# RMS norms of a hybrid decoder layer: squares summed in f32 on VectorE and two ones products a norm in the own tiles, where eight were

## The reference

```python
def rms_norm(x, g):
    y = x * lax.rsqrt(jnp.mean(x * x, axis=-1, keepdims=True) + EPS)
    return y * g

f1 = swiglu(rms_norm(h, ffn1_norm_pre), ffn1_w_in, ffn1_w_out)
h = h + 0.5 * rms_norm(f1, ffn1_norm_post)
u = rms_norm(h, mix_norm_pre)
...                       # u @ w_in: dilated windows A, sliding window B, memory attention M
merged = g_a * (o_a @ w_o_a) + g_b * (o_b @ w_o_b) + g_m * (o_m @ w_o_m)   # g: sigmoid(u @ w_gate + b)
h = h + rms_norm(merged @ w_out, mix_norm_post)
f2 = swiglu(rms_norm(h, ffn2_norm_pre), ffn2_w_in, ffn2_w_out)
h = h + 0.5 * rms_norm(f2, ffn2_norm_post)
```

## Time and profile before

| | us |
|---|---|
| runs (three) | 3924.27 median, 3917.88 to 3935.54 |
| the profiled execution | 3930.45 |
| its span on the slowest core (core 3) | 3928.9 |
| the spans of all cores | 3904.2 to 3928.9 |
| PE busy | 3747.7 (95%) |
| DVE, ACT, POOL busy | 1534.9 (39%), 1252.2 (32%), 305.7 (8%) |

### The profile page before, as it was taken

The page is one execution under the profiler, slowest core; times in us unless marked ns, Lnnn a source line. Parts: engine busy times, 40 slices in busy tenths (PEclk is TensorE's granted clock), DMA queues, the critical chain, the costliest instruction groups (busy, mean ns, idle before and its releaser), DMA issues.

```text
span 3928.9 us, 55392 instructions; the slowest of 8 cores (3904.2 to 3928.9 us)
## 1 busy us (share of the span) xinstructions
PE 3747.7 (95%) x19302; PEld 1820.2 (46%) x19302; DVE 1534.9 (39%) x2361; ACT 1252.2 (32%) x2011; POOL 305.7 (8%) x225
## 2 busy tenths in 40 slices
PE   7999998979999999999999999999999999999988
PEld 2444443544445444544454445444554455445533
DVE  2124322534225523542354334533453344433442
ACT  2123322243224422442234223422253225322421
POOL 0000100310003000300030003000300020001100
PEclk9999999999999999999999999999999999999989
DMA  9679999698434443434353445234524452344232
GB/s 217 149 150 201 205 206 192 179 143 205 145 135 144 154 152 133 157 140 145 134 177 118 142 144 192 107 130 153 196 78 154 154 194 92 140 155 165 77 132 98
DMA packets 93052, 597.96 MB, mean 152 GB/s; under 512 B 11120, under 2 KB 11248, under 8 KB 42608
## 3 DMA queue, kind: packets, MB, share of 16 engines
q1 hardware_dynamic: 86400, 538.53, 40.3%
q0 software_dynamic: 6384, 55.91, 10.9%
HBM read 616.21 MB, written 72.35 MB: 175 GB/s over the span
## 4 chain that ended last, share of the span: by engine, by line
PE 87%; DVE 5%; DMA 4%; issue 2%; ACT 2%; DVEq 0%; SPq 0%; ACTq 0%
PE ps L584 12%; PE ps L588 12%; PE ps L606 11%; PE pp L606 7%; PE pp L584 6%; PE pp L588 6%; PE ps L945 5%; PE ps L640 5%; DMA wslot<-wsc 3%; PE pp L640 3%; PE pp L945 2%; PE pp L485 2%; PE ps L681 2%; PE ps L949 2%; PE ps L981 2%
## 5 line engine op out<-in xcount | busy, mean ns | idle before, releaser
L584 PE MATMUL ps<-XN,wslot 128*128 128x512 bf16 x2424 | 578.5, 381 | 5.9 <-DVE XN L522 4.8
L588 PE MATMUL ps<-XN,wslot 128*128 128x512 bf16 x2432 | 579.0, 381 | 0.0
L606 PE MATMUL ps<-scr,wslot 128*128 128x512 bf16 x2134 | 476.3, 379 | 3.6 <-DMA wslot<-wsc 3.6
L595 DVE TENSOR_TENSOR scr<-scr,ps 128x512 bf16<-128x512 f32 x286 | 196.8, 688 | 616.8 <-PE ps L588 378.4
L584 PEld LDWEIGHTS ps<-XN,wslot 128*128 128x128 bf16 x2424 | 237.1, 98 | 295.8 <-issue 14.9
L588 PEld LDWEIGHTS ps<-XN,wslot 128*128 128x128 bf16 x2432 | 239.0, 98 | 289.7 <-issue 5.6
L668 POOL TENSOR_TENSOR ring<-scr 128x512 bf16<-128x512 f32 x78 | 140.9, 2012 | 2537.5 <-PE ps L658 1855.4
L593 ACT ACTIVATE scr<-ps 128x512 f32<-128x512 f32 x303 | 179.5, 593 | 482.3 <-PE ps L584 480.9
L606 PEld LDWEIGHTS ps<-scr,wslot 128*128 128x128 bf16 x2134 | 208.7, 98 | 255.3 <-issue 4.5
L606 PE MATMUL pp<-scr,wslot 128*128 128x512 bf16 x1210 | 271.0, 381 | 15.3 <-DMA wslot<-wsc 15.3
L945 PE MATMUL ps<-XN,wslot 128*128 128x512 bf16 x1024 | 246.8, 385 | 27.1 <-DMA wslot<-wsc 23.8
(11 more groups left out here) (141 smaller groups left out, 4316.4 us busy)
## 6 DMA issues: line engine op xcount, KB each, us to landing
wslot<-wsc SPq DMA_DIRECT2D x322, 1024.0 KB, 5.4
wslot<-wsc SPq DMA_DIRECT2D x144, 704.0 KB, 4.1
wslot<-wsc SPq DMA_DIRECT2D x58, 512.0 KB, 5.0
wsc<-wf POOLq DMA_DIRECT2D x28, 1024.0 KB, 15.8
X<-xT SPq DMA_DIRECT2D x22, 1024.0 KB, 7.5
yT<-X SPq DMA_DIRECT2D x16, 1024.0 KB, 7.3
wslot<-wf POOLq DMA_DIRECT2D x11, 1024.0 KB, 15.7
wsc<-wslot SPq DMA_DIRECT2D x11, 1024.0 KB, 12.7
```

What stands on the lines that cost most here:

```text
L584: P.add("pe", lambda e, c=c, b=bg_, half=half, wg=wg, xn=xn: e.matmul(ps[b][:], lhsT=wg[:, c, half * 128:(half + 1) * 128], rhs=xn[c], sta ...
L588: P.add("pe", lambda e, c=c, b=bu, half=half, wu=wu, xn=xn: e.matmul(ps[b][:], lhsT=wu[:, c, half * 128:(half + 1) * 128], rhs=xn[c], star ...
L595: P.add("dve", lambda e, s=s, b=bu, f=f, t=t: e.tensor_tensor(out=hid[t][:, f, :], in0=sg[:, s, :], in1=ps[b][:], op=ALU.mult), reads=[("s ...
L606: P.add("pe", lambda e, f=f, b=b, wo=wo, t=t: e.matmul(ps[b][:], lhsT=wo[:, f, :], rhs=hid[t][:, f, :], start=(f == 0), stop=(f == NF - 1) ...
```

## The change

In rounds 4 to 10 (`by_sums`) DVE adds the eight chunks of squares in f32 (`sum_add`; the first addition takes two bf16 squares, so seven additions), after the eighth ACT copies the sum to bf16 (`hi`), DVE subtracts that from the sum (`lo`, bf16), and PE multiplies the two by ones (`sum_mm`). The halo tiles, the memory tokens and the last round keep eight products. `post_steps` yields once before the "m" products instead of flushing them at its first step; `square_end` yields twice between the last addition and the "s" products. The rates change: both FFNs give 0.6 steps per input unit and per half output unit (before: one per input unit), gates 1.2 (before 1.1). The buffer `lnm` goes and Ln writes into rstd itself; the third square buffer is laid into the sums' memory.

```diff
+        by_sums = [False]
+        first_sq = {}
...
+        def sum_add(which, c, sq, ncols=TT):
+            ap, key = sq
+            _, ac, akey, _ = SUMS[which]
+            if c == 0:
+                first_sq[which] = sq
+                return
+            if c == 1:
+                a0, k0 = first_sq[which]
+                P.add("dve", lambda e: e.tensor_tensor(out=ac[:, 0:ncols], in0=a0, in1=ap, op=ALU.add), reads=[k0, key], writes=[akey])
+            else:
+                P.add("dve", lambda e: e.tensor_tensor(out=ac[:, 0:ncols], in0=ac[:, 0:ncols], in1=ap, op=ALU.add), reads=[akey, key], writes=[akey])
+            if c == 7:
+                hi, hk = sq_slot(which, ncols)
+                lo, lk = sq_slot(which, ncols)
+                P.add("act", lambda e: e.copy(out=hi, in_=ac[:, 0:ncols]), reads=[akey], writes=[hk])
+                P.add("dve", lambda e: e.tensor_tensor(out=lo, in0=ac[:, 0:ncols], in1=hi, op=ALU.subtract), reads=[akey, hk], writes=[lk])
+                first_sq[which] = ((hi, hk), (lo, lk))
+
+        def sum_mm(which, ncols=TT):
+            bank = SUMS[which][3]
+            for q, (ap, key) in enumerate(first_sq.pop(which)):
+                P.add("pe", lambda e, q=q, ap=ap: e.matmul(ps[bank][:, 0:ncols], lhsT=ones_s[:], rhs=ap, start=(q == 0), stop=(q == 1)),
+                      reads=["ones_s", key], writes=[bk(bank)])
...
             if early is None:
-                flush_tail()
+                if "m" in first_sq:
+                    yield
+                    sum_mm("m")
+                else:
+                    flush_tail()
                 stat_fin(BM, rstd_p, "rstd_p")
                 yield
...
             for c in range(8):
+                if pend and by_sums[0]:
+                    sum_add("s", *pend.pop(0))
...
+        def square_end(pend, ncols=TT):
+            if by_sums[0]:
+                sum_add("s", *pend.pop(0), ncols=ncols)
+                yield
+                yield
+                sum_mm("s", ncols)
+            while pend:
+                stat_mm(BS, *pend.pop(0), ncols=ncols)
...
                     P.add("dve", lambda e, o=o, b=b, F=F: e.tensor_copy(out=F[o], in_=ps[b][:]), reads=[bk(b)], writes=[F.key(o)])
+                    if by_sums[0]:
+                        sum_add("m", *pend.pop()[1:])
...
+            by_sums[0] = i + 1 < NTILE
...
-            rates = {"v": ("a", 0.6), "qk": ("a", 0.5), "gate1": ("b", 1.1), "gate2": ("b", 1.1)}
+            rates = {"v": ("a", 0.6), "qk": ("a", 0.5), "gate1": ("b", 1.2), "gate2": ("b", 1.2)}
...
-                run_phase(ffn(1, [xn_nxt], [bF[0]]), {"a": postmix(x_cur, xn_cur)}, {"in": ("a", 1)}, cast={"in": 0.3, "out": 0.2})
-                run_phase(ffn(2, [xn_cur], [bF[0]]), {"a": post1(x_nxt, xn_nxt)}, {"in": ("a", 1)})
+                run_phase(ffn(1, [xn_nxt], [bF[0]]), {"a": postmix(x_cur, xn_cur)}, {"in": ("a", 0.6), "out": ("a", 0.6)}, cast={"in": 0.3, "out": 0.2})
+                run_phase(ffn(2, [xn_cur], [bF[0]]), {"a": post1(x_nxt, xn_nxt)}, {"in": ("a", 0.6), "out": ("a", 0.6)})
```

More of the change, by code:

```diff
@@ L275, in build_program @@
         F0 = sb("F", [128, 8, TT], F32)
[L276 to L278 removed]
+        sqm = sb("sqm", [128, 2, TT], BF16)
+        sqs = sb("sqs", [128, 2, TT], BF16)
+        acm = sb("acm", [128, TT], F32)
+        acs = sb("acs", [128, TT], F32)
         rstd_p = sb("rstd_p", [128, TT], F32)
@@ L473, in build_program @@
         BM, BS = 7, 6
-        sq_ctr = {"m": 0, "s": 0}
-        def square(which, src_ap, src_key, ncols=TT):
-            buf = sqm if which == "m" else sqs
-            k = sq_ctr[which] % 3
-            sq_ctr[which] += 1
-            P.add("act", lambda e: e.activation(out=buf[:, k, 0:ncols], in_=src_ap, func=AF.Square), reads=[src_key], writes=[("sq" + which, k)])
-            return buf[:, k, 0:ncols], ("sq" + which, k)
+        SUMS = {"m": (sqm, acm, "acm", BM), "s": (sqs, acs, "acs", BS)}
@@ new lines, in build_program, with sq_slot @@
+        P.place("acs", ("acs", 0, 4 * TT))
+        P.place(("sqs", 2), ("acs", 0, 2 * TT))
+        P.place("acm", ("acm", 0, 4 * TT))
+        P.place(("sqm", 2), ("acm", 0, 2 * TT))
+        sq_ctr = {"m": 0, "s": 0}
+        by_sums = [False]
+        first_sq = {}
+        def sq_slot(which, ncols):
+            k = sq_ctr[which] % (2 if by_sums[0] else 3)
+            sq_ctr[which] += 1
+            buf, ac = SUMS[which][0:2]
+            if k == 2:
+                return ac[:, 0:TT // 2].bitcast(BF16)[:, 0:ncols], ("sq" + which, k)
+            return buf[:, k, 0:ncols], ("sq" + which, k)
@@ new lines, in sum_mm @@
+        def sum_mm(which, ncols=TT):
[3 more added lines that the diff above has]
+                      reads=["ones_s", key], writes=[bk(bank)])
+        def square(which, src_ap, src_key, ncols=TT):
+            ap, key = sq_slot(which, ncols)
+            P.add("act", lambda e: e.activation(out=ap, in_=src_ap, func=AF.Square), reads=[src_key], writes=[key])
+            return ap, key
@@ L488, in stat_fin @@
         def stat_fin(bank, rstd, rkey, ncols=TT):
-            P.add("act", lambda e: e.activation(out=lnm[:, 0:ncols], in_=ps[bank][:, 0:ncols], func=AF.Ln, bias=EPS, scale=1.0),
-                  reads=[bk(bank)], writes=["lnm"])
-            P.add("act", lambda e: e.activation(out=rstd[:, 0:ncols], in_=lnm[:, 0:ncols], func=AF.Exp, scale=-0.5),
-                  reads=["lnm"], writes=[rkey])
+            P.add("act", lambda e: e.activation(out=rstd[:, 0:ncols], in_=ps[bank][:, 0:ncols], func=AF.Ln, bias=EPS, scale=1.0),
+                  reads=[bk(bank)], writes=[rkey])
+            P.add("act", lambda e: e.activation(out=rstd[:, 0:ncols], in_=rstd[:, 0:ncols], func=AF.Exp, scale=-0.5),
+                  reads=[rkey], writes=[rkey])
         def post_steps(F, gain_ap, gkey, x, gidx=None, xn=None, early=None):
             if early is None:
-                flush_tail()
+                if "m" in first_sq:
[3 more added lines that the diff above has]
+                    flush_tail()
                 stat_fin(BM, rstd_p, "rstd_p")
@@ L508, in post_steps @@
                     pend.append((c, square("s", x[c], x.key(c))))
-                    if len(pend) > 2:
+                    if len(pend) > 2 and not by_sums[0]:
                         stat_mm(BS, *pend.pop(0))
@@ L512, in post_steps @@
             if xn is not None:
-                while pend:
-                    stat_mm(BS, *pend.pop(0))
+                for _ in square_end(pend):
+                    yield
                 for _ in norm_steps(x, gidx, xn):
                     yield
+        def square_end(pend, ncols=TT):
+            if by_sums[0]:
+                sum_add("s", *pend.pop(0), ncols=ncols)
+                yield
+                yield
+                sum_mm("s", ncols)
+            while pend:
+                stat_mm(BS, *pend.pop(0), ncols=ncols)
         def norm_steps(x, gidx, xn, ncols=TT):
@@ L529, in pre_steps @@
             for c in range(8):
+                if pend and by_sums[0]:
+                    sum_add("s", *pend.pop(0), ncols=ncols)
                 pend.append((c, square("s", x[c], x.key(c), ncols)))
-                if len(pend) > 2:
+                if len(pend) > 2 and not by_sums[0]:
                     stat_mm(BS, *pend.pop(0), ncols=ncols)
                 yield
-            while pend:
-                stat_mm(BS, *pend.pop(0), ncols=ncols)
+            for _ in square_end(pend, ncols):
+                yield
             for _ in norm_steps(x, gidx, xn, ncols):
```

5 lines of the change are left out of this document (2 added, 3 removed).

## The result

The changed kernel takes 3869.91 us (median of four executions, 3867.99 to 3878.79), 0.9872 of the kernel before, 95% interval [0.9856, 0.9887]. A second series gave 0.987 [0.9848, 0.9891]. The forecast was 3883 in a range of 3865 to 3904, faster.

A forecast was written before the change was run, and what follows sets the result against it. TensorE was taken to bound the kernel, busy 95% of the span. The terms -53.1 - 2.8 + 2.3 + 11.2 + 1.4 = -41.0 us gave 0.9896 of the profiled time, 3883 us on the median, range 3865 to 3904.

The forecast's parts named there:

- 252 products at 0.216 us, -53.1: 42 norms in tile rounds 4 to 10 lose six ones products each; six beside a transfer wait count nothing: -53.1 us.
- Waits beside the FFNs, -2.8: Beside the FFNs, 14 waits of the norms' last products, 2.8 us in all, disappear.
- Additions under cover at no cost: The norms' added DVE operations (232 us) and ACT copies (26 us) lie under PE's work and cost nothing.
- (a): FFN 2's output norm in the next v stage: PE waits 0.33 us for the second sum product, seven times, +2.3 us.
- (c): Gates: next FFN 1's input norm is summed one gate unit later, leaving DVE less catch-up: 0.2 x 7 = +1.4 us.
- (b): Rope stage: gain multiplies start 2.09 us later, PE waits 1.58 us in six tiles, 1.75 in one: +11.2 us.
- half clock: After attention's wait PE runs briefly at 1.2 GHz in each tile; not summed, 5 us allowed either way.
- first rival: No new rope-stage wait: DVE makes up the 2.09 us or the bank is needed later; 3870 us, chance 0.18.
- the paced steps end later in the FFNs: Both FFNs: side-work steps stretch from 18 of 22 input units to 35 of 38 half units; slower rival 3944, 0.05.

The follow-up runs named there:

- after: The changed kernel as profiled, against the kernel before: 3869.91 us median, 0.9872; its first profiled execution took 3878.79 us.
- the own product: Changed kernel, but FFN 2's output norm sums seven squares and the eighth has its own product (three products): 0.9873 and 0.9885 of the kernel before.
- the load back: Changed kernel with FFN 2's input-unit rate 0.7 instead of 0.6, so Ln precedes the last three silus: mean of cores 3879, executions 3883 to 3903 us.
- the vector work doubled: Changed kernel with one more same-size VectorE operation (a maximum) behind every running addition: 0.9951 of the kernel before.

## Why halo and last tile keep eight products

The changed kernel ran beside these as their measure:

> The changed kernel itself once more, as the measure for the three kernels beside it. By all theories its tile stages repeat: 14.75 us in the v stage, 42.2 to 42.5 in q and k, 76.84 and 37.99 beside the FFNs, 396.5 to 397.8 us a tile without half-clock extras; about 0.987 of the kernel before, and only the halo stretch (741 to 754 us, by core) differs between cores and runs.

It did repeat: 0.987, mean of cores 3863.

**Sums two halo tiles earlier.**

```diff
+by_sums[0] = True
 run_phase(ffn(1, [bXN[0]], [bF[0]]), {"a": post1(bXH, bXN[1]), "b": pre_steps(bX[1], 0, bXN[0])}, ...)
```

> The changed kernel with sums switched on two halo tiles earlier (third and fourth halo tile and the memory norm): 42 ones products fewer, six of them of half width. Theory 1 (there TensorE waits for weights from the DMA queues, so part of the time is taken up by longer waits): the products are worth at most 36 x 0.216 + 6 x 0.11 = 8.4 us; the mean of the cores falls by 2 to 6 us, tile stages from the second own tile on as in the changed kernel. Theory 2 (the halo tiles are as TensorE-bound as the own tiles): the full 8 us, less 1 for a low half that is waited for in the k and v projections.

> Sums in the last two halo tiles and a product of its own for the last square of FFN 2's norm, together. Theory 1: the two add up, 4 us in the tiles and 2 to 6 in the halo stretch by the mean of the cores, 0.998 of the changed kernel, 3860 us. Theory 2 (full worth in the halo, nothing in q and k): 8 us, all in the halo stretch.

Nothing gained: 0.9882 [0.9862, 0.9901], mean of cores 3865. From the first halo tile's v stage to the second own tile's, PE waits 26.6 us for transfers in the mean of the cores (32.6 and 30.2 in after's two profiles), but 17.0 at the ones products (4.8 and 4.7). Most of that is one wait beside the last halo tile's k and v projections, PE and then DVE:

```profile
710.61 0.58 PE L513 MATMUL pp<-sqs,ones_s 128*128 128x512 bf16 x1 [12.38 <-ACT sqs L506]
```
```profile
705.98 0.69 DVE L502 TENSOR_TENSOR acs<-acs,sqs 128x512 f32<-128x512 f32 x1 [0.55 <-ACT sqs L518]
...
709.01 0.69 DVE L502 TENSOR_TENSOR acs<-acs,sqs 128x512 f32<-128x512 f32 x1 [0.88 <-ACT sqs L518]
```

A step takes 3.03 us here, since each addition waits for ACT's square of the sum just made, and the projections offer a unit of 0.87 us a step. Both changes together (0.9861 [0.9837, 0.9886], mean 3858) show the same 12 us wait.

**Sums there, but not beside the projections**, with the own last product:

```diff
+by_sums[0] = False
 run_phase(kv_proj(3, ...), {"a": post1(bX[1], bXN[0])}, {"v": ("a", 1), "qk": ("a", 1)}, ...)
```

> Own product for the last square of FFN 2's norm, and sums in the last two halo tiles and the memory norm, but not in the norm beside the last halo tile's k and v projections, where the run before waited 12.7 us for the sum. 207 ones products (243 with the own product alone). Theory 1 (that one wait ate what the halo sums brought): the wait for sums in the projections is gone and the mean of the cores is 4 to 7 us under that of the kernel with the own product alone (3851 in its profile). Theory 2 (the halo stretch is set by the weights' transfers, and its waits fill up whatever is saved): the halo stretch keeps its 740 to 753 us.

0.9849 [0.9834, 0.9865], median 3861.32; its four executions (3858.55 to 3861.86) all lie under the fastest of the changed kernel's eight (3867.81), and the mean of cores is 3848 for 3863 (3855 and 3858 with the own product alone). The stretch from the first halo v stage to the second own tile's is 731.6 to 748.5 us by core, 737.6 in the mean (741.5 and 740.5 with the own product alone, 747.0 and 743.2 in after's two profiles). So 3 to 4 us come through of the 7.1 that 30 products of full and six of half width are worth. The wait in the projections is gone, as theory 1 had it, though with less than its 4 to 7 us. The rest does not go into transfer waits, as theory 2 had it: these are 27.4 us in that stretch, 29.6 and 28.4 with the own product alone. It goes into waits for the sums, 9.9 us at the ones products for 4.8, spread over the norms of the halo tiles, whose steps were not paced anew:

```profile
611.50 0.38 PE L517 MATMUL pp<-sqs,ones_s 128*128 128x512 bf16 x1 [1.20 <-ACT sqs L509]
612.30 0.38 PE L517 MATMUL pp<-sqs,ones_s 128*128 128x512 bf16 x1 [0.42 <-DVE sqs L510]
```

By its ratio and its mean of cores this is the fastest of the kernels here; the intervals of the own product and of both changes together overlap with its own.

**The last tile too.**

```diff
-by_sums[0] = i + 1 < NTILE
+by_sums[0] = True
```

> The changed kernel with sums in the last tile too: 18 ones products fewer. There nothing runs beside the norms (TensorE waits 18 us for the w_out norm, and the norm behind FFN 2 ends the kernel). Theory 1 (the saved products are free only where something covers the additions): the inner norm after w_out runs at VectorE's pace, which gets 8 additions of 0.61 more, and each of the three norms gets a chain of addition, copy and subtraction of about 2 us; the last tile gets 7 to 10 us longer (308.0 in the changed kernel), the time as much. Theory 2 (the products set those norms' ends): 18 x 0.216 = 3.9 us less.

Two executions compare, 3890.12 and 3891.42. The last tile takes 323.3 us for 308.0, 15 us more where I expected 7 to 10. PE waits for the inner norm after w_out, whose steps go through DVE and ACT in turn with nothing of PE's beside them:

```profile
3728.70 0.59 PE L513 MATMUL pp<-sqs,ones_s 128*128 128x512 bf16 x1 [26.40 <-ACT sqs L506]
```
```profile
3708.92 0.69 DVE L500 TENSOR_TENSOR acs<-sqs 128x512 f32<-128x512 bf16 x1 [0.82 <-ACT sqs L518]
...
3711.95 0.69 DVE L502 TENSOR_TENSOR acs<-acs,sqs 128x512 f32<-128x512 f32 x1 [0.88 <-ACT sqs L518]
```

Again 3.03 us a step: to the addition of 0.61 comes a wait of 0.88 for the square, which I had left out.

## The prediction, step by step

- *252 products at 0.216 us, -53.1:* right. Every stage lost what its products cost, and the first own tile's six, beside the transfer wait of the earlier trace rows, can't be told from that wait's spread (gates of that tile 86.3 to 89.3 us by core before, 86.5 to 89.3 after).
- *Waits beside the FFNs, -2.8:* right; 2.2 to 2.7 us of them are gone by core, 2.3 on most, and none came.
- *Additions under cover at no cost:* right, and in the FFNs with room for twice as many. In the gates the cover is thinner than the text said.
- *(a) v stage, 0.33 us seven times:* right, 0.35 (once 0.63), 2.7 us.
- *(c) gates, +1.4:* right in size, +1.5. That the unit fewer is the whole cause is argued: with the own product, which leaves this norm alone, w_out takes 14.49 in every tile. The w_out row of after, as the earlier trace rows, with 0.52 us of idle (0.81 in every other tile) where it had 0.39:

```profile
1718.03 4.26 PE L1038 MATMUL ps<-scr,wslot 128*128 128x512 bf16 x19 [0.52 <-DVE scr L1025]
```

- *(b) rope stage, +11.2: this step failed.* It came to 3.2 us. The term began "The table load of Ln starts 0.46 us after the last product's start and DVE's first gain multiply 2.72 us after that", with durations read from before. The load was no longer there. The rest of it stood: DVE's 13.67 us to the first rope multiply (13.66 in after, 1965.93 to 1979.59), the lateness at the eleventh unit (in four tiles of seven at the tenth too; with the load back also at the fifth, 0.6 to 1.0 us), DVE's L717 as the releaser, and, with the load put back, 1.52 to 1.95 us a tile for the 1.58 forecast. The forecast term less the load's 1.28 us is 0.30: three tiles of after wait 0.29 to 0.31 us, the other four 0.52 to 0.66, and why these wait longer stays open. The first rope multiply, and a unit that waits, 2.23 us after the one before where 1.94 is gapless:

```profile
1979.59 0.69 DVE L717 TENSOR_TENSOR scr<-ps,scr 128x512 f32<-128x512 f32 x1
...
1991.99 1.89 PE L697 MATMUL ps<-XN,wslot 128*128 128x512 bf16 x8
...
1994.22 1.89 PE L697 MATMUL ps<-XN,wslot 128*128 128x512 bf16 x8
```

With the measured terms the sum is -53.1 - 2.3 + 2.7 + 3.2 + 1.5 = -48.0, against 48 in the means of cores. That they agree so closely is in part luck: by the mean of the cores the own tiles of the two profiles differ by 46.4 us, about the 48.0 less the 1.7 at half clock, which the prediction allowed for and could not sum, and the rest of the 48 comes from the stretch ahead of them, which varies by more than that. The other 3.7 us between the two profiled executions lie on their slowest cores in the stretch with the transfer waits, 12.2 us shorter where its products explain 7.8 at most. The first rival's 3870 was met in time, by luck: it named other reasons. DVE made up nothing, it had less to make up. The prediction saw that the paced steps end later in the FFNs but not that this moves Ln past the last silu; the table that ACT holds at a stage's end is part of what an order moves.

## What to carry over

Work taken from the bound engine is worth its start-to-start price wherever that engine runs gapless, and what it is replaced by is free only where the steps between are paced for its whole chain: here 3.03 us a norm step through ACT and DVE. Where a norm's end lies on a stage boundary, send the last chunk by itself instead of through the sum. Where norms get sums, pace their steps anew, or waits for the sums eat half of the gain, as in the halo tiles. When steps are re-paced, count the ACT_TABLE_LOADs: an Ln that moves past the last silu spares one in the next stage.

## What the hardware showed unexpectedly

- An ACTIVATE starts right behind its ACT_TABLE_LOAD (1959.41 + 1.28 to 1960.70). The Trainium skill (ScalarE: Activation LUTs, § What ACT_TABLE_LOAD costs) adds a drain of 1.38 us to every switch, 2.66 in all; putting the load back cost 1.28 us at the gain multiply and no more than 1.30 a tile on PE, so no drain shows here.
- A DVE addition of two SBUF tiles stretches from 0.69 to 2.27 us beside GpSimd's additions, a multiply that reads PSUM does not.
- Cores that do the same work differ by 25 us in the profile of before (3904.2 to 3928.9), and the stretch that waits for weights by 19 of it (746.6 to 765.7); own tiles 2 to 7 together take 2424.0 to 2427.9 us there.
- A wait of PE can cost more than its length: with the vector work doubled, 2.5 to 3.1 us of idle among the gates are followed by a stretch at half clock in five tiles of six, for 1.8 to 2.0 us more; with the own product, which takes away the waits in the v stage and nearly all in the q and k stage, the six tiles have 21 us at half clock and not 39.
